# Adding the residual into the PSUM sums before the last slabs, with row sums on ScalarE and VectorE, in a three-layer mixer and expert network

## The chip, the cores and the metric

The kernel runs on one core of a Trainium2 chip. The metric is the device time of one execution in microseconds. TensorE does all the matrix products, VectorE and ScalarE the elementwise work, GpSimd a part of the splitting of weights, and SyncE issues every DMA.

## The reference

256 tokens of width 1024 pass through two Transformer-like layers with layer norm after each part, and then through a third layer with RMS norm. Each layer has a mixer and a PEER block, in which every token picks 8 x 16 of 16384 single-neuron experts.

```python
# first block: two layers, DN_ALPHA = 4 ** 0.25
h = layer_norm(DN_ALPHA * h + mix, ln_g[layer, 0], ln_b[layer, 0])
ffn = peer(h, w_q[layer], sub_keys[layer], u_tab[layer], v_tab[layer])
h = layer_norm(DN_ALPHA * h + ffn, ln_g[layer, 1], ln_b[layer, 1])
...
# second block: one layer, 16 meta tokens ahead of the 256
h = h + hybrid_mixer(rmsnorm(h, g_mix), ...)
h = h + peer_ffn(rmsnorm(h, g_ffn), ...)
h = rmsnorm(h, g_final)
```

So each of the six stages ends in a sum over a long inner dimension (`mix` or `ffn`), a residual, and a norm over the 1024 columns of each token. `layer_norm` takes the mean off, multiplies by the gain, divides by the root of the variance and adds the bias; `rmsnorm` has no mean and no bias.

## The kernel before

**Stages.** The six stages run one after the other: `ab`, `peer0`, `c`, `peer1`, `s`, `peer2`. The mixers are `ab`, `c` and `s`. Weights stream from HBM in slabs of 128x1024 floats through a ring of three buffers. For full precision each slab is split in two: ScalarE copies `ring` to `w_hi` (`split_lead`, L829), then GpSimd or VectorE forms `w_lo = ring - w_hi` (`split_rest`, L527). Activations are split likewise (`x_hi`, `x_lo`, or `c_hi`, `c_lo`), and each product is three matmuls: hi with hi (L576), hi with lo (L577), lo with hi (L578). A ring buffer may be refilled when its `w_lo` is ready, and `w_hi` rewritten when TensorE has counted the slab that used it (`slab_used`).

**Column slabs and row slabs.** Column slabs (`features`) are the weights that multiply x: 8 chunks x 3 matmuls of 256 columns into one bank `col`. Row slabs (`rows`) close a stage: for two token tiles t and two column halves they add 3 matmuls of 512 columns to each of the four PSUM banks `acc0` to `acc3`, 12 matmuls a slab. A stage ends with 8 (`ab_out`, `c_out`), 16 (`s_out`) or 128 (`v0` to `v2`) row slabs. In the last two slabs of a stage (`row_tail`) TensorE does tile 0 of both slabs first, then `acc2`, then `acc3`, so that tile 0 is full four bank sums ahead of the end.

**The joint between two stages.** When tile 0 is full, VectorE adds the residual to each bank (L1105, which also yields the row sum), forms the mean (L1129), multiplies the centred values by the gain in place in PSUM (L1137), and ScalarE sums the squares of the centred values (L889). Variance (L1141), root (ScalarE, L872), reciprocal (L1116) and the scaling with the bias into `h` (L1146) follow. TensorE transposes `h` (L664) into the `acc` banks, ScalarE copies them to `x_hi` (L865), VectorE forms `x_lo` (L1089), and the first column slab of the next stage can begin. TensorE fills the time with matmuls whose result nobody reads (`keep_busy`, L633). At the joint from `peer1` to `s`, RMS squares and scalings (L1212) of the new `h` come behind the layer norm, ahead of the transposes. Behind `s` and behind `peer2` only the RMS norm stands (`finish_rms`); there the residual is added into `h` in SBUF, and the squares are taken from `h`.

**Order.** Every engine runs its own program in written order. Nothing is scheduled at run time; semaphores join the engines. In the `v` slabs of a peer stage VectorE alternates `split_rest` and `coef_rest` (L1245, `c_lo`), while GpSimd is idle. In the mixers' row slabs GpSimd splits the weights, and VectorE makes `c_hi` and `c_lo` (`coef`, L1236 and L1238).

## Time and profile before

| | us |
|---|---|
| median of 3 runs | 2907.55 (2906.78 to 2907.93) |
| span of the profiled execution | 2904.1 |
| TensorE busy in it | 2869.2 (99%) |
| VectorE, ScalarE, GpSimd busy | 1934.1, 1562.2, 894.8 |

The page gives the span from the first to the last instruction; its own whole time isn't in it, and the median of the runs lies 3.45 us above the span. The page is read from the busy shares, through the waits of TensorE, to the timelines of single joints. The timeline gives for each instruction its start, its duration and the idle time in front of it with what ended that. A matmul's duration includes its passage through the array, so the distance between two starts tells its rate.

### The profile page before, as it was taken

The page shows a single profiled execution, that of the slowest core. Times are in us where ns is not written, and L with a number is a line of the kernel's source. Part 1 is how long each engine was busy: PE and PEld are TensorE (multiplying, and loading weights), DVE is VectorE, ACT ScalarE, POOL GpSimd, SP SyncE. Part 2 cuts the span into 40 slices and gives each one's busy share as a digit, 9 for nine tenths or more (in the row PEclk, how much of TensorE's full clock was granted, in tenths as well). Part 3 has the DMA queues.
Part 4 walks back from the last instruction along what each step waited for, and adds up shares of the span by engine and source line. Part 5 has one row for each costly group of instructions (what it writes and reads, how often), then busy time and mean ns, then how long its engine had stood idle before and what let it go on. Part 6 is the DMA issues. An engine that isn't in the chain of part 4 may idle for free.

```text
span 2904.1 us, 59734 instructions
## 1 busy us (share of the span) xinstructions
PE 2869.2 (99%) x21539; PEld 2620.1 (90%) x21539; DVE 1934.1 (67%) x3382; ACT 1562.2 (54%) x2548; POOL 894.8 (31%) x361
## 2 busy tenths in 40 slices
PE   8999999999999999999999999999999999999999
PEld 7899999888888889999998888889899999988887
DVE  4388577787556536947778855675539667788655
ACT  4444444677455554444467745554544544577554
POOL 3689600000004368970000000265779910000000
PEclk9999999999999999999999999999999999999999
DMA  6566655555765556665555576433565665555664
GB/s 214 163 184 184 185 168 172 173 176 174 240 192 158 151 160 182 184 185 170 170 174 174 175 238 192 151 128 127 164 192 181 182 181 167 173 175 176 207 193 161
DMA packets 146464, 515.20 MB, mean 177 GB/s; under 512 B 17552, under 2 KB 18576, under 8 KB 146336
## 3 DMA queue, kind: packets, MB, share of 16 engines
q1 hardware_dynamic: 146336, 513.46, 56.9%
q8 instruction: 85, 1.39, 0.2%
q14 instruction: 43, 0.35, 0.0%
HBM read 509.20 MB, written 4.19 MB: 177 GB/s over the span
## 4 chain that ended last, share of the span: by engine, by line
PE 90%; DVE 3%; ACT 2%; POOL 2%; issue 2%; DMA 1%; SPq 0%; DVEq 0%; ACTq 0%; POOLq 0%
PE col L576 15%; PE col L578 15%; PE col L577 15%; PE acc L576 13%; PE acc L578 13%; PE acc L577 13%; POOL w_lo L527 2%; PE col L723 2%; PE acc L723 2%; PE acc L683 1%; ACT w_hi L829 1%; ACT work L889 0%; PE acc L2301 0%; PE misc L2314 0%; DVE acc L1105 0%
## 5 line engine op out<-in xcount | busy, mean ns | idle before, releaser
L527 POOL TENSOR_TENSOR w_lo<-ring,w_hi 128x1024 fp32r<-128x1024 f32 x357 | 894.6, 2515 | 1442.5 <-ACT w_hi L829 1441.8
L829 ACT ACTIVATE w_hi<-ring 128x1024 fp32r<-128x1024 f32 x941 | 993.6, 1056 | 533.3 <-PE acc L578 439.3
L576 PE MATMUL col<-x_hi,w_hi 128*128 128x256 f32 (+1 forms) x3976 | 1125.0, 283 | 5.1 <-DVE x_lo L1089 3.6
L577 PE MATMUL col<-x_lo,w_hi 128*128 128x256 f32 (+1 forms) x3976 | 1118.9, 281 | 0.0
L578 PE MATMUL col<-x_hi,w_lo 128*128 128x256 f32 (+1 forms) x3976 | 1118.4, 281 | 0.0
L527 DVE TENSOR_TENSOR w_lo<-ring,w_hi 128x1024 fp32r<-128x1024 f32 x584 | 714.2, 1223 | 379.0 <-ACT w_hi L829 375.6
L576 PEld LDWEIGHTS col<-x_hi,w_hi 128*128 128x128 f32 x3976 | 750.7, 189 | 9.4 <-issue 6.2
L578 PEld LDWEIGHTS col<-x_hi,w_lo 128*128 128x128 f32 x3976 | 751.7, 189 | 0.0
L577 PEld LDWEIGHTS col<-x_lo,w_hi 128*128 128x128 f32 x3976 | 747.5, 188 | 0.7
L576 PE MATMUL acc<-w_hi,c_hi 128*128 128x512 f32 x1664 | 653.5, 393 | 1.0 <-issue 1.0
L578 PE MATMUL acc<-w_hi,c_lo 128*128 128x512 f32 x1664 | 648.3, 390 | 0.0
L577 PE MATMUL acc<-w_lo,c_hi 128*128 128x512 f32 x1664 | 647.3, 389 | 0.0
L836 ACT ACTIVATE work<-col 128x256 f32 (+1 forms) x464 | 178.7, 385 | 716.6 <-PE col L578 716.5
L578 PEld LDWEIGHTS acc<-w_hi,c_lo 128*128 128x128 f32 x1664 | 312.3, 188 | 66.0
L576 PEld LDWEIGHTS acc<-w_hi,c_hi 128*128 128x128 f32 x1664 | 312.5, 188 | 64.8 <-issue 1.5
L577 PEld LDWEIGHTS acc<-w_lo,c_hi 128*128 128x128 f32 x1664 | 312.6, 188 | 63.3
L1245 DVE TENSOR_TENSOR c_lo<-work,c_hi 128x256 fp32r<-128x256 f32 x390 | 165.5, 425 | 14.3 <-ACT c_hi L994 14.0
L994 ACT ACTIVATE c_hi<-work 128x256 fp32r (+1 forms) x384 | 153.6, 401 | 0.0
L1252 DVE MAX8 work<-work 128x8 f32<-128x128 f32 (+1 forms) x144 | 35.4, 323 | 166.1 <-ACT work L951 165.8
L1378 DVE SCALAR_TENSOR_TENSOR work<-acc,work 128x512 f32 (+1 forms) x96 | 61.9, 686 | 100.4 <-PE acc L723 100.4
L1367 DVE TENSOR_TENSOR h_tok<-mask_i,pairs_of_gate 128x2048 f16<-128x2048 f16 x96 | 123.7, 1288 | 0.2 <-issue 0.2
L999 ACT ACTIVATE h_tok<-iota_fp,neg_i 128x128 f16<-128x128 f16 x384 | 121.8, 388 | 0.2
(303 smaller groups left out, 1870.3 us busy)
## 6 DMA issues: line engine op xcount, KB each, us to landing
ring<-in_u SPq DMA_DIRECT2D x384, 512.0 KB, 3.7
ring<-in_v SPq DMA_DIRECT2D x384, 512.0 KB, 3.6
ring<-in_wq SPq DMA_DIRECT2D x48, 512.0 KB, 3.7
ring<-in_s_in SPq DMA_DIRECT2D x21, 512.0 KB, 3.4
ring<-in_c_in SPq DMA_DIRECT2D x16, 512.0 KB, 3.7
ring<-in_s_out SPq DMA_DIRECT2D x16, 512.0 KB, 3.3
...
```

The costliest lines, as they stand in the source:

```text
L527: eng.tensor_tensor(k.w_lo[s.slot][:, :], k.ring[s.slot][:, :], k.w_hi[s.slot][:, :].bitcast(F32), ALU.subtract).then_inc(k.lo[s.slot], 1)
L576: pe.matmul(out, a[0], b[0], start=start, stop=False, **kw)
L577: pe.matmul(out, a[0], b[1], start=False, stop=False, **kw)
L578: return pe.matmul(out, a[1], b[0], start=False, stop=stop, **kw)
L723: ins = pe.matmul(banks[t // HALF][:, t % HALF * EARLY:(t % HALF + 1) * EARLY], k.oh1[:, t, :], k.oh2[:, n, t, :], start=n == 0, stop=n == ...
L829: act.activation(k.w_hi[s.slot][:, :], k.ring[s.slot][:, :], ACT.Copy).then_inc(k.hi[s.slot], 1)
L836: act.activation(dst, src, func).then_inc(k.evac, 1)
L994: act.activation(k.c_hi[s.slot][:, :], act_of[:, s.index(values), :], ACT.Copy).then_inc(k.coef_h, 1)
L999: act.activation(k.oh1[:, t, :], k.iota_b[:, :], ACT.Abs, bias=k.neg_i1[:, at])\
L1245: dve.tensor_tensor(k.c_lo[s.slot][:, :], src, k.c_hi[s.slot][:, :].bitcast(F32), ALU.subtract).then_inc(k.coef[s.slot], 1)
L1367: dve.tensor_tensor(k.oh2.rearrange("p n t (i two) -> p n t i two", two=2), mask.unsqueeze(1).to_broadcast(shape), k.gate[:, bass.ds(b.ind ...
L1378: ins = dve.scalar_tensor_tensor(part, banks[half][:, :].rearrange("p (t i) -> p i t", t=HALF), 1.0 / GATE_UNIT, part, ALU.mult, ALU.mult)
```

## The change

Seven things are changed.

1. `ADDS` is 4 and `TAIL` is 6. In the last six row slabs of each stage, the four slabs ahead of the last two carry a mark 0 to 3. TensorE signals `bank_done` when bank number mark has been summed in that slab, and VectorE adds the residual into that bank right there, from PSUM to PSUM, and signals `resid`. TensorE waits for residual number n before its next sum into bank n: slab end-5 waits ahead of bank 0, slab end-4 ahead of bank 1, slab end-3 ahead of bank 2, and the tail ahead of bank 3.
2. On VectorE the residual n stands behind the splits or coefficients of slab end-4+n. It reads `h` from SBUF and the bank.
3. The loop over slabs on TensorE and on VectorE has one round fewer, and the slabs left stand behind it in straight order.
4. The row sums of banks 0, 1 and 3 come from ScalarE (a copy with an accumulator), that of bank 2 from VectorE (`tensor_reduce`).
5. Centring goes from PSUM to `h` in SBUF, and the scaling goes from `h` to `h`. The centring and scaling of the two tiles are interleaved. In `finish` ScalarE does tile 0's root between the tiles; ahead of `s` both further weight splits now stand behind the second root.
6. Behind `s` and `peer2` the squares and the RMS scaling read the banks; behind `s` VectorE also copies the banks into `h`.
7. The first column slab of a stage does its 16 products with `x_hi` first and its 8 products with `x_lo` last, with a wait for each part. There are fewer filler matmuls in a joint (8 and 8 in place of 12 and 20; 6 and 8 in place of 8 and 16 ahead of `s`).

```diff
+    def fresh_features(self, out, hi, lo, cols):
+        quads = (range(0, DC // 2), range(DC // 2, DC))
+        for quad, tiles in zip(quads, (3, 1), strict=True):
+            w.next(k.xhi, tiles)
+            for c in quad:
+                pe.matmul(out, hi[:, c, :], k.x_hi[:, c, cols], start=c == 0, stop=False)
+                pe.matmul(out, lo[:, c, :], k.x_hi[:, c, cols], start=False, stop=False)
+        for quad in quads:
+            w.next(k.x_ready, 2)
+            for c in quad:
+                ins = pe.matmul(out, hi[:, c, :], k.x_lo[:, c, cols], start=False, stop=c == DC - 1)
...
@@ def rows
+                bank = t * 2 + half
+                if mark and bank == mark - 1:
+                    self.w.next(k.resid)
...
+                if bank == mark and bank < ADDS - 1:
+                    ins.then_inc(k.bank_done, 1)
...
@@ def row_tail
-        self.row_slab(Slab(end - SLOTS))
+        for bank in range(begun, ADDS):
+            self.row_slab(Slab(end - TAIL + bank), mark=bank)
...
@@ def finish (ScalarE)
+        self.row_sum(0, 0)
+        self.row_sum(0, 1)
+        self.centred_squares(0)
+        self.w.next(k.tile_full)
+        act.wait_ge(k.used, end)
+        self.row_sum(1, 1)
+        self.tile_std(0, eps)
         if after != ("s",):
-            for t in range(NT):
-                self.centred_squares(t)
-            for t in range(NT):
-                self.tile_std(t, eps)
+            self.centred_squares(1)
+            self.tile_std(1, eps)
             self.split_lead(Slab(end + 1))
...
         else:
-            for t in range(NT):
-                self.centred_squares(t)
-                if t:
-                    self.tile_std(0, eps)
-                self.split_lead(Slab(end + 1 + t))
+            self.centred_squares(1)
             self.tile_std(1, eps)
+            for n in range(1, SLOTS):
+                self.split_lead(Slab(end + n))
             self.lead_meta()
...
@@ def residual (VectorE)
+        if bank < ADDS - 1:
+            self.w.next(k.bank_done)
+        else:
+            dve.wait_ge(k.used, last - 1)
...
+        dve.scalar_tensor_tensor(acc, h, alpha, acc, ALU.mult, ALU.add).then_inc(k.resid, 1)
...
@@ def layer_norm
         def centre(t, half):
-            self.w.next(k.sq)
-            dve.wait_ge(k.mean, means + t + 1)
-            acc = k.acc[t * 2 + half][:, :]
-            own.do(dve.scalar_tensor_tensor(acc, acc, k.small[:, 20 + t:21 + t], gain[:, half * 512:(half + 1) * 512],
-                                            ALU.add, ALU.mult))
+            if half == 0:
+                w.next(k.mean)
+                w.next(k.sq)
+            cut = slice(half * 512, (half + 1) * 512)
+            own.do(dve.scalar_tensor_tensor(k.h[:, t, cut], k.acc[t * 2 + half][:, :], k.small[:, 20 + t:21 + t],
+                                            gain[:, cut], ALU.add, ALU.mult))
...
-        def scale(t, half):
-            cut, acc = slice(half * 512, (half + 1) * 512), k.acc[t * 2 + half][:, :]
-            dve.scalar_tensor_tensor(k.h[:, t, cut], acc, k.small[:, 12 + t:13 + t], bias[:, cut], ALU.mult, ALU.add)\
-               .then_inc(k.rms_in if rms_next else k.h_part, 1)
+        def scale(t, half, after):
+            cut = slice(half * 512, (half + 1) * 512)
+            own.join(after)
+            dve.scalar_tensor_tensor(k.h[:, t, cut], k.h[:, t, cut], k.small[:, 12 + t:13 + t], bias[:, cut],
+                                     ALU.mult, ALU.add).then_inc(k.rms_in if rms_next else k.h_part, 1)
...
@@ def finish_rms
+        self.w.next(k.sq)
+        keep(0, 0)
+        self.mean_square(0, 1)
+        keep(0, 1)
+        self.w.next(k.sq)
+        keep(1, 0)
+        self.rms_norm(0, slot, summed=True)
+        self.mean_square(1, 1)
+        keep(1, 1)
+        self.rms_norm(1, slot, summed=True)
...
@@ MixAB.vector (the same line in MixC and MixS)
             e.coef(self.y[:, n, :], Slab(out + n))
+            if n >= 8 - ADDS:
+                e.residual(n - (8 - ADDS), out + 7, DN_ALPHA)
```

TensorE at slab 3 of the eight of `ab_out`, whose `w_hi1` it uses, between the transposes of `y` (L1579, now L1644). Before:

```order
L1579 MATMUL misc<-ident,work 128x128 [waits ret_y,ab_wide]
L1579 MATMUL misc<-ident,work 128x128 x3
L576 MATMUL acc0<-w_hi1,c_hi1 128x512 [waits lo_ready1,coef_ready1]
L577 MATMUL acc0<-w_lo1,c_hi1 128x512
L578 MATMUL acc0<-w_hi1,c_lo1 128x512
```

Now:

```order
L1644 MATMUL misc<-ident,work 128x128 [waits ret_y,ab_wide]
L1644 MATMUL misc<-ident,work 128x128 x3
L581 MATMUL acc0<-w_hi1,c_hi1 128x512 [waits residual_in_bank,lo_ready1,coef_ready1]
L582 MATMUL acc0<-w_lo1,c_hi1 128x512
L583 MATMUL acc0<-w_hi1,c_lo1 128x512
```

The slab's first matmul has a third semaphore to wait for, `residual_in_bank`.

VectorE in the same stretch. `c_hi2` and `c_lo2` in the first two rows are slab 4's coefficients, made from `y`, which TensorE transposes and ScalarE copies (`y_ready`). Before:

```order
L1236 CAST c_hi2<-work 128x256 [waits slab_used,y_ready]
L1238 TENSOR_TENSOR c_lo2<-work,c_hi2 128x256 [waits coef_hi_ready]
L1236 CAST c_hi0<-work 128x256 [waits slab_used]
L1238 TENSOR_TENSOR c_lo0<-work,c_hi0 128x256 [waits coef_hi_ready]
L1236 CAST c_hi1<-work 128x256 [waits slab_used,y_ready]
L1238 TENSOR_TENSOR c_lo1<-work,c_hi1 128x256 [waits coef_hi_ready]
L1236 CAST c_hi2<-work 128x256 [waits slab_used]
L1238 TENSOR_TENSOR c_lo2<-work,c_hi2 128x256 [waits coef_hi_ready]
```

Now:

```order
L1299 CAST c_hi2<-work 128x256 [waits slab_used,y_ready]
L1301 TENSOR_TENSOR c_lo2<-work,c_hi2 128x256 [waits coef_hi_ready]
L1159 SCALAR_TENSOR_TENSOR acc0<-h_tok,acc0 128x512 [waits slab_added_to_bank]
L1299 CAST c_hi0<-work 128x256 [waits slab_used]
L1301 TENSOR_TENSOR c_lo0<-work,c_hi0 128x256 [waits coef_hi_ready]
L1159 SCALAR_TENSOR_TENSOR acc1<-h_tok,acc1 128x512 [waits slab_added_to_bank]
L1299 CAST c_hi1<-work 128x256 [waits slab_used,y_ready]
L1301 TENSOR_TENSOR c_lo1<-work,c_hi1 128x256 [waits coef_hi_ready]
L1159 SCALAR_TENSOR_TENSOR acc2<-h_tok,acc2 128x512 [waits slab_added_to_bank]
L1299 CAST c_hi2<-work 128x256 [waits slab_used]
L1301 TENSOR_TENSOR c_lo2<-work,c_hi2 128x256 [waits coef_hi_ready]
L1159 SCALAR_TENSOR_TENSOR acc3<-h_tok,acc3 128x512 [waits slab_used]
```

Residual 0, which slab 3 on TensorE waits for, stands behind slab 4's coefficients; residuals 1 to 3 stand behind those of slabs 5 to 7.

VectorE at the end of the layer norm behind `c` (L1137, now L1184, is the centring; L1146, now L1201, the scaling). Before:

```order
L1137 SCALAR_TENSOR_TENSOR acc2<-acc2,small,work 128x512 [waits mean_ready,squares_ready]
L1137 SCALAR_TENSOR_TENSOR acc3<-acc3,small,work 128x512 [waits mean_ready,squares_ready]
L1141 TENSOR_SCALAR small<-small 128x1
L1116 RECIPROCAL small<-small 128x1 [waits std_ready,dve_step]
L1146 SCALAR_TENSOR_TENSOR h_tok<-acc0,small,work 128x512 [waits dve_step]
L1146 SCALAR_TENSOR_TENSOR h_tok<-acc1,small,work 128x512
L1116 RECIPROCAL small<-small 128x1 [waits std_ready]
L1146 SCALAR_TENSOR_TENSOR h_tok<-acc2,small,work 128x512 [waits dve_step]
L1146 SCALAR_TENSOR_TENSOR h_tok<-acc3,small,work 128x512
```

Now:

```order
L1195 RECIPROCAL small<-small 128x1 [waits std_ready]
L1201 SCALAR_TENSOR_TENSOR h_tok<-h_tok,small,work 128x512 [waits dve_step]
L1184 SCALAR_TENSOR_TENSOR h_tok<-acc2,small,work 128x512 [waits squares_ready,mean_ready]
L1190 TENSOR_SCALAR small<-small 128x1 [waits squares_ready]
L1201 SCALAR_TENSOR_TENSOR h_tok<-h_tok,small,work 128x512 [waits dve_step]
L1184 SCALAR_TENSOR_TENSOR h_tok<-acc3,small,work 128x512
L1195 RECIPROCAL small<-small 128x1 [waits std_ready]
L1201 SCALAR_TENSOR_TENSOR h_tok<-h_tok,small,work 128x512 [waits dve_step] x2
```

The four scalings read `h_tok` in place of a bank, and the first of them stands ahead of tile 1's centring.

ScalarE at the same joint (L829, now L860, writes `w_hi`; L889, now L928, squares; L872, now L903, takes the root). Before:

```order
L829 ACTIVATE w_hi0<-ring0 128x1024 [waits slab_loaded0,slab_used]
L889 ACTIVATE work,small<-acc0,small 128x512 [waits squares_ready,mean_ready]
L889 ACTIVATE work,small<-acc1,small 128x512 [waits squares_ready]
L889 ACTIVATE work,small<-acc2,small 128x512 [waits squares_ready,mean_ready]
L889 ACTIVATE work,small<-acc3,small 128x512 [waits squares_ready]
L872 ACTIVATE small<-small 128x1 [waits variance_ready] x2
L829 ACTIVATE w_hi1<-ring1 128x1024 [waits slab_loaded1,slab_used]
```

Now:

```order
L860 ACTIVATE w_hi0<-ring0 128x1024 [waits slab_loaded0,slab_used]
L910 ACTIVATE work,small<-acc0 128x512 [waits tile_summed_in_psum]
L910 ACTIVATE work,small<-acc1 128x512
L928 ACTIVATE work,small<-acc0,small 128x512 [waits squares_ready,mean_ready]
L928 ACTIVATE work,small<-acc1,small 128x512 [waits squares_ready]
L910 ACTIVATE work,small<-acc3 128x512 [waits slab_used,tile_summed_in_psum]
L903 ACTIVATE small<-small 128x1 [waits variance_ready]
L928 ACTIVATE work,small<-acc2,small 128x512 [waits squares_ready,mean_ready]
L928 ACTIVATE work,small<-acc3,small 128x512 [waits squares_ready]
L903 ACTIVATE small<-small 128x1 [waits variance_ready]
L860 ACTIVATE w_hi1<-ring1 128x1024 [waits slab_loaded1,slab_used]
```

Three row sums (L910) are new ahead of and between the squares; `w_hi1` follows the second root as before.

## Rows read from the trace of the kernel before

**Rows 1.** the page: busy us of each engine, share of the span

```profile
PE 2869.2 (99%) x21539; PEld 2620.1 (90%) x21539; DVE 1934.1 (67%) x3382; ACT 1562.2 (54%) x2548; POOL 894.8 (31%) x361
```

**Rows 2.** waits: TensorE line, its releaser, us in total, times, longest

```profile
PE acc L664 <- DVE h_tok L1146: 3.7, 6, 1.0
```

**Rows 3.** timeline, TensorE, joint c to peer1: start, duration, row, idle before

```profile
1045.79 1.48 PE L633 MATMUL col<-ident 128*128 128x256 bf16 x12
...
1050.95 1.31 PE L664 MATMUL acc<-ident,h_tok 128*128 128x128 f32 x8 [1.04 <-DVE h_tok L1146]
...
1054.62 0.36 PE L576 MATMUL col<-x_hi,w_hi 128*128 128x256 f32 x1 [0.85 <-DVE x_lo L1089]
```

**Rows 4.** timeline, VectorE at the same joint

```profile
1043.27 0.70 DVE L1105 SCALAR_TENSOR_TENSOR acc<-h_tok,acc 128x512 f32<-128x512 f32 x1 [4.49 <-PE acc L578]
...
1049.94 0.16 DVE L1116 RECIPROCAL small<-small 128x1 f32<-128x1 f32 x1
1050.14 1.41 DVE L1146 SCALAR_TENSOR_TENSOR h_tok<-acc,small,work 128x512 f32<-128x512 f32 x2
...
1051.65 1.41 DVE L1146 SCALAR_TENSOR_TENSOR h_tok<-acc,small,work 128x512 f32<-128x512 f32 x2
1052.98 2.69 DVE L1089 TENSOR_TENSOR x_lo<-acc,x_hi 128x512 fp32r<-128x512 f32 x4
```

**Rows 5.** timeline, ScalarE and then GpSimd at the same joint

```profile
1044.95 0.69 ACT L889 ACTIVATE work<-acc,small 128x512 f32<-128x512 f32 x1 [3.35 <-DVE small L1129]
...
1045.76 0.69 ACT L889 ACTIVATE work<-acc,small 128x512 f32<-128x512 f32 x1
...
1050.26 1.04 ACT L829 ACTIVATE w_hi<-ring 128x1024 fp32r<-128x1024 f32 x1
...
1053.15 1.25 ACT L865 ACTIVATE x_hi<-acc 128x512 fp32r<-128x512 f32 x2 [0.26 <-PE acc L664]
...
1051.38 2.36 POOL L527 TENSOR_TENSOR w_lo<-ring,w_hi 128x1024 fp32r<-128x1024 f32 x1 [7.30 <-ACT w_hi L829]
```

**Rows 6.** timeline, VectorE and then TensorE, fifth slab from the end of peer0

```profile
887.82 0.42 DVE L1245 TENSOR_TENSOR c_lo<-work,c_hi 128x256 fp32r<-128x256 f32 x1
...
888.02 0.39 PE L576 MATMUL acc<-w_hi,c_hi 128*128 128x512 f32 x1
```

**Rows 7.** timeline, ab_out slab 3: TensorE, GpSimd, VectorE

```profile
78.79 0.48 PE L576 MATMUL acc<-w_hi,c_hi 128*128 128x512 f32 x1
...
79.17 2.40 POOL L527 TENSOR_TENSOR w_lo<-ring,w_hi 128x1024 fp32r<-128x1024 f32 x1 [0.21 <-ACT w_hi L829]
...
80.25 1.46 DVE L1236 CAST c_hi<-work 128x256 fp32r<-128x256 f32 x1
81.75 0.43 DVE L1238 TENSOR_TENSOR c_lo<-work,c_hi 128x256 fp32r<-128x256 f32 x1
```

**Rows 8.** timeline, VectorE beside GpSimd, ahead of s and entering c

```profile
1850.77 1.27 DVE L1222 SCALAR_TENSOR_TENSOR work<-work,small 16x1024 f32<-16x1024 f32 x1
...
1851.56 2.74 POOL L527 TENSOR_TENSOR w_lo<-ring,w_hi 128x1024 fp32r<-128x1024 f32 x1 [556.97 <-ACT w_hi L829]
...
911.50 2.27 DVE L1953 TENSOR_TENSOR work<-work 128x8 f32<-128x8 f32 x1
...
911.34 2.40 POOL L527 TENSOR_TENSOR w_lo<-ring,w_hi 128x1024 fp32r<-128x1024 f32 x1 [1.70 <-ACT w_hi L829]
```

**Rows 9.** timeline, TensorE, joint peer1 to s

```profile
1854.24 0.66 PE L653 MATMUL misc<-ident,work 16*128 16x16 f32 x8
...
1867.82 0.36 PE L576 MATMUL col<-x_hi,w_hi 128*128 128x272 f32 x1 [0.84 <-DVE x_lo L1089]
```

**Rows 10.** windows: stretch, us, busy per engine (PE to POOL), clock, DMA

```profile
64.00:66.00 2.00, 2.00 (x6) 1.56 (x5) 1.05 (x3) 0.00 (x0) 0.00 (x0) 0.50 0.35 143
```

**Rows 11.** timeline, TensorE and then VectorE, the end of the kernel

```profile
2896.91 0.39 PE L578 MATMUL acc<-w_hi,c_lo 128*128 128x512 f32 x1
...
2900.28 1.42 DVE L1212 SCALAR_TENSOR_TENSOR work<-h_tok,small,work 128x512 f32<-128x512 f32 x2
```

More of the change, by code:

```diff
@@ L899, in tile_squares, with summed_squares @@
         self.tile_std(t)
+    def summed_squares(self, t, last):
+        k = self.k
+        for half in range(2):
+            if half == 0:
+                self.w.next(k.tile_full)
+            elif t:
+                self.act.wait_ge(k.used, last + 1)
+            self.square(k.acc[t * 2 + half][:, :], 2 * t + half)
+        self.tile_std(t)
     def finish(self, name, end):
@@ L1120, in layer_norm @@
         k, dve, own = self.k, self.dve, self.own
+        w = self.w
         gain, bias = view(k.big, G_AT[slot], D), view(k.big, G_AT[slot] + D, D)
-        means = self.w.count(k.mean)
-        def residual(t, half):
-            self.add_residual(t, half, last, DN_ALPHA, sums=True)
+        own.join()
         def minus_mean(t):
-            own.join()
+            w.next(k.sums, 2 if t == 0 else 2)
             dve.tensor_scalar(k.small[:, 20 + t:21 + t], k.small[:, 16 + 2 * t:17 + 2 * t],
@@ L1438, in peer @@
         at = first + EARLY + SLOTS
-        with dve.Fori(0, (VREST - SLOTS) // SLOTS) as i:
+        with dve.Fori(0, (VREST - SLOTS - ADDS) // SLOTS) as i:
             for p in range(SLOTS):
                 value(Slab(at + p, i))
-        for n in range(KEYS - (VREST - SLOTS) % SLOTS, KEYS):
-            value(Slab(first + n))
+        alpha = 1.0 if f"peer{layer}" in RMS_AFTER else DN_ALPHA
+        for bank in range(ADDS):
+            value(Slab(first + KEYS - ADDS + bank))
+            self.residual(bank, first + KEYS - 1, alpha)
 def vector_program(k, dve):
@@ L2099, in vector @@
             e.coef(yT, Slab(out + n))
+            if n >= 8 - ADDS:
+                e.residual(n - (8 - ADDS), out + 7, DN_ALPHA)
 class MixS:
```

136 lines of the change are left out of this document (74 added, 62 removed).

## Prediction

> **What bounds the kernel now.** I read the busy times first: TensorE works 2869.2 of 2904.1 us [rows 1], so time is lost or won only where TensorE stands still, in steps of a microsecond. The view of waits shows where: the transposes behind the four layer norms wait 3.7 us in all, six times [rows 2], in the joints between stages. So I laid the timelines of one joint side by side, and count in it from the start of the fillers, 1045.79, when the last slab has been fed; the first column slab starts at 1054.62, **8.83 us** on [rows 3]. The reader is to see in the rows that every link waits for the one before it, so that a link that moves by 0.1 moves the end by 0.1. The chain inside: residual from -2.52 (1043.27), reciprocal at 4.15, scaling of tile 0 at 4.35 and of tile 1 at 5.86, `x_lo` from 7.19 [rows 4]. From tile 1's scaling to its `x_hi` it is 1.50, and each `x_hi` takes 0.63 [rows 4, 5]. The joints behind `ab` and `peer0` repeat this within 0.1.
>
> **The joint after the change, times on the same count.** Residuals are already in, so ScalarE starts the row sums at -2.52. I price one at the 0.81 by which the squares follow each other [rows 5]: ended by -0.93. Mean, 0.25; tile 0's squares from -0.65 to 0.94; row sum of bank 3 to 1.75; mean; tile 1's squares from 2.02 to 3.61 (they cannot start before the last bank is summed). VectorE's small steps cost 0.12 to 0.2 each (reciprocal to scaling, 0.20 [rows 4]): variance 3.64, tile 0's second scaling 3.76, centring of bank 3 4.43, reciprocal 5.10, tile 1's scaling **5.29**, half a microsecond earlier than 5.86. With `x_hi` products first TensorE needs only the third `x_hi`: 5.29 + 1.50 + 0.63 + a restart. The restart lies between 0.06 (second scaling of a pair of 1.41 to the transposes) and 0.27 (second `x_lo`, 1054.35, to 1054.62) [rows 3, 4]; I take 0.2. That is 7.62 in place of 8.83: **a gain of 1.2** per layer norm if nothing else comes in. The `x_lo` parts no longer set the start: four of 0.67 behind the last scaling [rows 4] are done 1.8 after that start, and are first wanted when two thirds of the slab's 24 products are done.
>
> **The port.** Something does come in. ScalarE writes `w_hi` of the next slab right behind the second root: today at 1050.26, and GpSimd's split begins 1.12 later, 1051.38, and lasts 2.36 [rows 5]. After the change the root comes at 3.83, `w_hi` at 4.03, and GpSimd's split at 5.15 to 7.51, around tile 1's scaling at 5.29. Today that scaling runs under GpSimd's split unharmed, two in 1.41 [rows 4, 5], but it reads a bank and one SBUF tensor. Now it reads `h` and the bias, two SBUF tensors. Rows 8 show what such a pair does: VectorE's 128x8 sum of two SBUF tensors, begun 0.16 behind GpSimd's split, took 2.27 us and ended with it (913.77 against 913.74); and when VectorE's scaling of two SBUF tensors had begun first (1850.77 to 1852.04), GpSimd's split took 2.74 in place of 2.40 [rows 8]. The Trainium skill (SBUF — State Buffer, section Who interferes with whom) says that a VectorE instruction with two SBUF inputs contends with a GpSimd instruction that reads SBUF, and that the later one waits until the first has finished. By that rule centring into SBUF is what hurts in this change; the trace agrees in both directions.
> So tile 1's first scaling waits until 7.51 and the first matmul comes at 7.55 + 2.33 = 9.88: **1.05 slower** than now. If VectorE wins the race by 0.1, GpSimd gets in between its two scalings, the first quad starts at 7.6, but the second `x_hi` of tile 1 comes at 10.5, and the slab ends within 0.2 of the same time. The bounds of this term are -1.2 (no blocking) and +1.3. Three joints (behind `ab`, `peer0`, `c`): **+3.15**.
>
> **Ahead of s.** The same block holds tile 1's scaling; and both weight splits now stand behind the second root, so GpSimd has a second split waiting. VectorE's next instructions with two SBUF inputs (the sum of the squares, the second scaling) fall behind that one. Chain: scaling 7.5 to 8.15, GpSimd to 10.5, sum and variance 10.75, second scaling to 11.5, tile 0 normed 11.7 to 13.0, tile 1's squares end 12.6, its variance 13.2, normed from 13.8, first matmul at 13.8 + 2.33 = 16.15. Today it is 1867.82 - 1854.24 = 13.58 [rows 9]: **+2.6**. Without blocking the chain gives 13.35, -0.25; these are the bounds.
>
> **The wait in the peer stages.** Residual 0 stands on VectorE behind the coefficients of slab end-4. In `peer0` those begin at 887.82, and slab end-5, which must not touch bank 0 before the residual, begins at 888.02 [rows 6]. So TensorE stands: 887.82 + 0.38 (the next instruction starts at or just ahead of the end of one of 0.42) + 0.70 (the residual as now [rows 4]) + 0.2 restart = 889.10, **1.08**. In `peer1` and `peer2` the same two rows lie equally close. The later residuals have the cover of the slab that came late: residual 1 ends near 891.5, and bank 1 of the next slab is due a quarter into it, near 892.5. Three peer stages: **+3.25**. Bounds 2.7 and 3.6.
>
> **The wait in ab.** Here VectorE is late. Slab 3 begins on TensorE at 78.79. Residual 0 stands behind slab 4's coefficients, whose copy begins at 80.25 and is held to 81.71 by GpSimd's split (79.17 to 81.57), and whose `c_lo` begins at 81.75 [rows 7]. Residual 0: 82.10 to 82.80; slab 3 at 83.0 in place of 78.79: **4.2**. What hung on slab 3 moves along: the split of slab 6, the second transposes, `y_ready`, slab 6's copy (again behind a split), residual 2 at about 90.8 against bank 2 of slab 5, due at 90.65: 0.3. In sum **+4.5**; bounds 3.8 (the later copies find the port free) and 6.5 (one more split lies across). In `c` and `s` the coefficients come a third of a slab after the slab begins, and residual 0 is done 1 us ahead of its use: nothing.
>
> **Behind s and peer2.** At the end, the RMS scaling of tile 1 starts at 2900.28; the last matmul is issued at 2896.91, so the count begins at 2897.14 [rows 11], and it is 3.14. Now the squares start at -2.52 on the bank, tile 1's first ends at 0.4, tile 0 is scaled 0.6 to 1.9, tile 1 from 2.74: **-0.4**; GpSimd is idle there. Behind `s` three copies of 0.67 on VectorE take the gain and more, and `x_hi` first gives it back: 0, bounds -0.4 and +0.5. One loop round fewer costs nothing: its slabs are the same instructions. The fillers that are left out ran in time that had no other use.
>
> **The sum.** 3.15 + 2.6 + 3.25 + 4.5 - 0.4 = **+13.1 us**. It is made on the profiled span, 2904.1, and carried to the median, which lies 3.45 above it: 2907.55 + 13.1 = **2920.7**. A measurement of this kernel can tell about 0.2% (5.8 us) from no change: faster means below 2901.7, slower above 2913.4.
>
> **Rivals.**
> A. *The clock falls.* TensorE now stands 3.2 us in each layer norm joint, with fewer fillers before, and 4.0 in `ab`. At 64 to 66 us the granted clock is 0.50 (1.2 GHz), behind 32 small matmuls [rows 10]; while that lasts TensorE does half its work, so a fall of 2 to 4 us costs 1 to 2; I take 1.5. In one to five places: 2922 to 2928. For it: the gaps are three times the 1.04 that stands ahead of the transposes now [rows 3]. Against it: ahead of each gap the engine is busy without a pause. The Trainium skill (TensorE: Matmul & The Clock Gate, Part 1) says the gate follows how busy the engine has been; no run here shows a fall behind a plain gap. By the rule A is what would happen if the gaps count as idle. Chance 20% (two falls or more).
> B. *The port doesn't block a scaling.* Only the 128x8 sum was seen to wait, not this form. Then the joints give 3 x -1.2 and -0.25, and the two waits stay: +3.5, 2911, within 0.2%. 10%.
> C. *Not slower: the residuals don't hold TensorE and the port doesn't block.* VectorE would have to reach residual 0 ahead of the slab, that is 1.1 us earlier in the peers and 4.2 in `ab`; rows 6 and 7 speak against both. -3.6 - 0.25 - 0.4 = -4.3: 2903.3. It decides at 0 in both. 4%; 3% for a gain beyond 0.2% by something not seen here.
> D. *ab waits less or more* by 2: 2918 to 2923, inside the forecast.
>
> **How the numbers follow.** The forecast with its own width (2916 to 2923) 58%, A 20%, B 10%, C 4%, a gain 3%, beyond 2929 5%. The range takes in A and B: 2910.5 to 2928. Faster 0.03, the same 0.16 (B, C and the low edge), slower 0.81.
>
> **What would show it.** In the new profile: (1) TensorE idle for residuals once in each peer stage, about 1 us, and once in `ab` for 4 us; if VectorE's residual ends before the slab begins, those steps are wrong. (2) Scalings of 2.5 to 3 us in place of 0.7 while GpSimd splits, in four joints; if they take 0.7, B is right. (3) The first matmul 9.9 behind the last slab, 16 ahead of `s`. (4) Granted clock of 1.0 in all joints; a 0.5 gives A.

## The result, and the profile after

The changed kernel takes **2924.73 us** (median of five runs, 2921.02 to 2930.06) against 2907.55 (2904.75 to 2908.67) for the kernel before on the same chip: ratio 1.0063, 95% interval 1.0052 to 1.0074. It is slower by 17.2 us where the sum said 13.1; the time lies inside the range given, 4.0 us above the forecast. It is outside the forecast's own width (2916 to 2923) and inside that of rival A (2922 to 2928). The profiled execution is the longest of the five, 2930.06, with a span of 2928.2; so its difference to the span before, 24.1 us, holds more than the medians show.

TensorE's waits in the changed kernel, beside [rows 2] (TensorE line, its releaser, us in total, times, longest):

```profile
PE acc L690 <- DVE h_tok L1201: 12.1, 6, 2.9
PE acc L581 <- DVE acc L1159: 6.7, 5, 4.0
PE acc L690 <- DVE work L1275: 3.8, 4, 2.4
PE col L659 <- DVE h_tok L1201: 3.5, 1, 3.5
```

The wait behind the scalings (L690, which was L664) grew from 3.7 to 12.1 us, and the wait for residuals (L1159) is new. Joint behind `peer0`, TensorE, then VectorE, then GpSimd, to be laid beside [rows 3 to 5]:

```profile
912.54 1.05 PE L659 MATMUL col<-ident 128*128 128x256 bf16 x8
914.31 1.05 PE L659 MATMUL col<-ident 128*128 128x256 bf16 x8 [0.72 <-DVE small L1176]
...
917.12 0.66 PE L690 MATMUL acc<-ident,h_tok 128*128 128x128 f32 x4 [1.30 <-DVE h_tok L1201]
920.70 1.97 PE L690 MATMUL acc<-ident,h_tok 128*128 128x128 f32 x8 [2.93 <-DVE h_tok L1201]
```

```profile
916.32 0.74 DVE L1201 SCALAR_TENSOR_TENSOR h_tok<-h_tok,small,work 128x512 f32<-128x512 f32 x1
...
917.83 2.82 DVE L1201 SCALAR_TENSOR_TENSOR h_tok<-h_tok,small,work 128x512 f32<-128x512 f32 x1
```

```profile
917.76 2.34 POOL L532 TENSOR_TENSOR w_lo<-ring,w_hi 128x1024 fp32r<-128x1024 f32 x1 [6.88 <-ACT w_hi L860]
```

One line, L1201, takes 0.74 without GpSimd beside it and 2.82 when it starts 0.07 behind GpSimd's split. While TensorE stands for it, the granted clock falls (windows: stretch, us, TensorE busy, clock, DMA share, GB/s):

```profile
914.00:916.00 2.00, 1.51 (x12) 1.00 0.02 4
916.00:918.00 2.00, 0.66 (x4) 1.00 0.01 4
918.00:920.00 2.00, 0.00 (x0) 0.69 0.00 0
920.00:922.00 2.00, 1.30 (x6) 0.50 0.42 100
922.00:924.00 2.00, 2.00 (x10) 0.50 0.41 162
924.00:926.00 2.00, 2.00 (x13) 0.61 0.00 0
```

At 0.50 (1.2 GHz) the transposes take 1.97 in place of 1.31 and the first slab's products come every 0.21 us in place of 0.12. The same fall follows in the joints behind `ab` and `c`, ahead of `s`, and in `ab` at 82 to 90 us. One at 62 us is in the kernel before too, half as long. One more, inside `s` at 1929 to 1933, follows a wait for ScalarE that the change has no part in; the kernel before has that wait as well, and its clock stays at 1.0 there. TensorE inside `s`, changed and before:

```profile
1928.95 0.80 PE L2338 MATMUL acc<-ident,work 128*128 128x128 f32 x3 [3.07 <-ACT work L2446]
```

```profile
1907.00 0.55 PE L2269 MATMUL acc<-ident,work 128*128 128x128 f32 x3 [2.69 <-ACT work L2377]
```

TensorE in `ab`, where slab 3 stood at 78.79 before [rows 7], and at the fifth slab from the end of `peer0` [rows 6]:

```profile
79.77 0.63 PE L1644 MATMUL misc<-ident,work 128*128 128x128 f32 x4 [0.27 <-DVE work L1757]
84.38 0.76 PE L581 MATMUL acc<-w_hi,c_hi 128*128 128x512 f32 x1 [3.98 <-DVE acc L1159]
84.94 0.63 PE L582 MATMUL acc<-w_lo,c_hi 128*128 128x512 f32 x1
```

```profile
898.85 0.47 PE L581 MATMUL acc<-w_hi,c_hi 128*128 128x512 f32 x1 [0.81 <-DVE acc L1159]
```

Ahead of `s` the scaling and then a 128x1 sum are held, each by one of two splits in a row (VectorE, GpSimd):

```profile
1876.82 2.83 DVE L1201 SCALAR_TENSOR_TENSOR h_tok<-h_tok,small,work 128x512 f32<-128x512 f32 x1
1879.56 2.30 DVE L1258 TENSOR_TENSOR small<-small 128x1 f32<-128x1 f32 x1
```

```profile
1876.74 5.10 POOL L532 TENSOR_TENSOR w_lo<-ring,w_hi 128x1024 fp32r<-128x1024 f32 x2 [4.79 <-ACT w_hi L860]
```

**Where the 24.1 us of span went.** Five joints and the end are counted from the last row slab (start of the fillers; ahead of `s`, of the meta tokens' transposes) to the first column matmul; stages are what lies between.

| us | before | after | moved |
|---|---|---|---|
| joint ab to peer0 | 8.81 | 9.35 | +0.54 |
| joint peer0 to c | 8.91 | 10.06 | +1.15 |
| joint c to peer1 | 8.83 | 9.77 | +0.94 |
| joint peer1 to s | 13.58 | 15.75 | +2.17 |
| joint s to peer2 | 6.18 | 5.81 | -0.37 |
| behind the last slab | 6.96 | 6.39 | -0.57 |
| start and ab | 93.31 | 101.42 | +8.11 |
| peer0, c, peer1, s, peer2 | 799.50, 135.26, 799.62, 223.56, 799.58 | 801.77, 136.10, 803.43, 227.77, 800.58 | +12.13 |

Of the 20.2 us in the stages, the waits for residuals are some 7.5 (3.98 and 0.29 in `ab`, about 1.05 with the restart in each peer stage). The rest, nearly 13 us, has no wait of that size behind it; the windows show it as time at half clock. I add up, over all windows of 2 us, 2 us times what the clock lacks of 1.0, and call it the clock's deficit: 5.0 us before, **22.6** after. A part of it falls on time in which TensorE stands anyway and costs nothing; 0.8 to 3.3 us of each deficit lie behind the last matmul.

### The profile page after: what moved, and what is told of

The parts are those of the page before. It is cut to its first block, busy times and chain, and to the rows that moved or that the text cites. A ratio compares the mean times of both kernels' runs of the same rounds, so it can differ in the third digit from the quotient of the medians.

```text
span 2928.2 us, 59587 instructions
## 1 busy us (share of the span) xinstructions
PE 2876.2 (98%) x21481; PEld 2626.8 (90%) x21481; DVE 1942.7 (66%) x3374; ACT 1568.2 (54%) x2572; POOL 894.9 (31%) x361
## 3 DMA queue, kind: packets, MB, share of 16 engines
q8 instruction: 86, 1.41, 0.2%
## 4 chain that ended last, share of the span: by engine, by line
PE 90%; DVE 3%; POOL 2%; ACT 2%; issue 2%; DMA 1%; SPq 0%; DVEq 0%; ACTq 0%; POOLq 0%
PE col L581 15%; PE col L583 15%; PE col L582 15%; PE acc L581 13%; PE acc L583 13%; PE acc L582 13%; POOL w_lo L532 2%; PE col L749 2%; PE acc L749 2%; ACT w_hi L860 1%; PE acc L709 1%; DVE h_tok L1201 1%; PE acc L690 0%; DVE h_tok L1184 0%; PE acc L2370 0%
## 5 line engine op out<-in xcount | busy, mean ns | idle before, releaser
L860 ACT ACTIVATE w_hi<-ring 128x1024 fp32r<-128x1024 f32 x941 | 993.5, 1056 | 546.8 <-PE acc L583 455.8
L581 PE MATMUL col<-x_hi,w_hi 128*128 128x256 f32 (+1 forms) x3928 | 1111.8, 283 | 1.6 <-POOL w_lo L532 1.2
L582 PE MATMUL col<-x_lo,w_hi 128*128 128x256 f32 (+1 forms) x3928 | 1106.0, 282 | 0.0
L583 PE MATMUL col<-x_hi,w_lo 128*128 128x256 f32 (+1 forms) x3928 | 1105.5, 281 | 0.0
L581 PEld LDWEIGHTS col<-x_hi,w_hi 128*128 128x128 f32 x3928 | 742.4, 189 | 4.8 <-issue 2.9
L583 PEld LDWEIGHTS col<-x_hi,w_lo 128*128 128x128 f32 x3928 | 743.3, 189 | 0.0
L582 PEld LDWEIGHTS col<-x_lo,w_hi 128*128 128x128 f32 x3928 | 739.2, 188 | 0.7
```

What stands on the lines that cost most here:

```text
L581: pe.matmul(out, a[0], b[0], start=start, stop=False, **kw)
L582: pe.matmul(out, a[0], b[1], start=False, stop=False, **kw)
L583: return pe.matmul(out, a[1], b[0], start=False, stop=stop, **kw)
L860: act.activation(k.w_hi[s.slot][:, :], k.ring[s.slot][:, :], ACT.Copy).then_inc(k.hi[s.slot], 1)
```

## The experiments

Each ran in five rounds beside the kernel before (medians 2907.10, 2907.02 and 2908.16 in the three groups, the ratios each to its own). An interval is about 0.12% wide to either side, 3.5 us, so differences of one or two microseconds between the runs are read in the traces. Two groups differ by up to 1.1 us in the kernel before alone. A trace is one execution and has chance falls of the clock of its own: the one at 62 us lasts 6.8 us in some traces, 3.4 in others, and is missing in three. The joints, in us, in the order `ab`, `peer0`, `c`, `peer1`, `s`:

| kernel | median us, ratio (interval) | joints | deficit |
|---|---|---|---|
| before | 2907.55 | 8.81 8.91 8.83 13.58 6.18 | 5.0 |
| changed | 2924.73, 1.0063 (1.0052-1.0074) | 9.35 10.06 9.77 15.75 5.81 | 22.6 |
| e1 centring in PSUM | 2915.98, 1.0029 (1.0018-1.0039) | 7.24 7.53 7.70 15.31 5.81 | 10.4 |
| e10 late split | 2916.24, 1.0035 (1.0022-1.0049) | 7.25 7.98 7.67 15.75 5.81 | 15.0 |
| e6 order ahead of s | 2919.96, 1.0047 (1.0033-1.0060) | 9.49 10.06 9.77 11.16 5.80 | 16.3 |
| e4 fillers | 2916.88, 1.0035 (1.0023-1.0047) | 9.33 9.61 9.33 15.31 5.81 | 4.9 |
| e3 ab | 2920.08, 1.0044 (1.0030-1.0057) | 9.76 10.05 9.79 15.78 5.81 | 18.3 |
| e2 all residuals early | 2929.17, 1.0073 (1.0059-1.0087) | 9.78 9.08 9.78 15.76 5.80 | 18.9 |
| e7 residual 0 early | 2923.68, 1.0060 (1.0046-1.0074) | 9.78 10.06 9.78 15.78 5.80 | 17.9 |
| e9 before, fewer fillers | 2911.92, 1.0019 (1.0010-1.0029) | 9.29 9.55 8.83 14.34 6.17 | 11.0 |
| e11 before, x_hi first | 2903.74, 0.9988 (0.9979-0.9997) | 8.11 8.17 8.11 12.84 5.67 | 3.0 |
| e8 all mended | 2898.95, 0.9968 (0.9956-0.9980) | 7.23 7.54 7.25 11.15 5.80 | 2.8 |
| e12 e8, fewer fillers | 2904.66, 0.9987 (0.9978-0.9996) | 7.24 7.53 7.24 11.14 5.81 | 12.5 |

**Centring left in PSUM.**

```diff
-            own.do(dve.scalar_tensor_tensor(k.h[:, t, cut], k.acc[t * 2 + half][:, :], k.small[:, 20 + t:21 + t],
+            own.do(dve.scalar_tensor_tensor(k.acc[t * 2 + half][:, :], k.acc[t * 2 + half][:, :], k.small[:, 20 + t:21 + t],
...
-            dve.scalar_tensor_tensor(k.h[:, t, cut], k.h[:, t, cut], k.small[:, 12 + t:13 + t], bias[:, cut],
+            dve.scalar_tensor_tensor(k.h[:, t, cut], k.acc[t * 2 + half][:, :], k.small[:, 12 + t:13 + t], bias[:, cut],
```

> The changed kernel, but the centred values stay in the PSUM banks and the second scaling reads a bank and one SBUF tensor, as in the kernel before. All else, the order included, is the changed kernel. Theory (GpSimd's split holds every VectorE instruction with two SBUF inputs): the scalings take 0.7 us in place of 2.8 and 3.5 for a pair, the first column matmul stands 7.6 to 7.9 us behind the last row slab in place of 9.4 to 10.1 behind ab, peer0 and c, and 13.4 to 14.2 in place of 15.75 ahead of s. That is 3 x 2.1 + 2 = 8 us; TensorE's gaps shrink from 2.9 to under 1, so the falls of the granted clock at these four joints go too, 1 to 2 us each: 2924.7 - 8 - 4 = 2912.5 us (2909 to 2917). Rival 1 (the scaling is long because it reads what the centring has just written to SBUF, or for another reason that is not GpSimd): the same rows must be examined; if a two-SBUF instruction elsewhere beside a split is unharmed, this falls. Rival 2 (the fewer filler matmuls are what lowers the clock, not the gaps): joints shorten by 8 us, but the clock still falls: 2916.5 us.

At the joint behind `c`, VectorE and GpSimd:

```profile
1052.53 1.41 DVE L1201 SCALAR_TENSOR_TENSOR h_tok<-acc,small,work 128x512 f32<-128x512 f32 x2
```

```profile
1052.46 2.36 POOL L532 TENSOR_TENSOR w_lo<-ring,w_hi 128x1024 fp32r<-128x1024 f32 x1 [6.65 <-ACT w_hi L860]
```

The split begins 0.07 ahead of the scalings, as in the changed kernel, and two of them take 1.41. The three joints shorten by 2.1 to 2.5. Ahead of `s` the expectation was wrong, 15.31 for 13.4 to 14.2: the 128x1 sum, whose inputs lie in SBUF in either kernel, now meets the splits (2.18 us, in a wait of TensorE of 4.07). The clock still falls behind `c`, ahead of `s`, inside `s` and in `ab`, though not behind `ab` or `peer0`. Median 2915.98: inside the range written down, but no nearer to the theory's 2912.5 than to rival 2's 2916.5 (joints shorter, clock still falling), and the trace has some of each. In the trace 4.3 us of the difference are in `ab`, which the edit doesn't touch.

**The same block from the other side, and ahead of s.** In one run the weight copy that releases GpSimd moves behind tile 0's `x_hi` in three joints; in the other both copies ahead of `s` move behind the `x_hi` of tile 0 and of tile 1. Centring through SBUF stays in both.

```diff
-            self.split_lead(Slab(end + 1))
             self.lead_x([0])
+            self.split_lead(Slab(end + 1))
             self.lead_x([1])
```

> The changed kernel, with ScalarE's weight copy of the next slab, which releases GpSimd's split, moved behind the x_hi copies of tile 0 in the joints behind ab, peer0 and c. Centring and scaling still go through SBUF. Theory (GpSimd's split is what holds the scaling): the pair of scalings takes 1.4 us in place of 3.5, the first column matmul comes 7.2 to 7.8 us behind the zero in place of 9.4 to 10.1, the gap of 2.9 us falls under 1 us: 3 x 2.1 = 6.3 us, and the clock falls of three joints, about 1.5 us each, go or shrink: 2924.7 - 6.3 - 3 = 2915.4 us (2912 to 2918). Rival (two SBUF inputs alone make it long): the pair still takes 3.5 us, no gain. Rival 2 (w_lo of the second column slab is now late): a wait of up to 1 us at that slab takes half the gain.

```diff
-            for n in range(1, SLOTS):
-                self.split_lead(Slab(end + n))
...
-            self.lead_x(range(NT), at=META)
+            for t in range(NT):
+                self.lead_x([t], at=META)
+                self.split_lead(Slab(end + 1 + t))
```

> The changed kernel, with one thing moved on ScalarE at the joint from peer1 to s alone: the two weight copies that release GpSimd's splits stand behind the copies of x_hi of tile 0 and of tile 1, not behind the second root. VectorE's centring and scaling still read two SBUF tensors. Theory: with no split running there, the scaling of 2.83 us and the 128x1 sum of 2.30 us take 0.7 and 0.2, and ScalarE's squares no longer stand behind 2 us of copies; the first column matmul comes 11.4 to 12.5 us behind the zero in place of 15.75, and the granted clock stays at 1.0 there: 2924.7 - 3.8 - 1.7 = 2919.2 us. Rival 1 (two SBUF inputs are slow for another reason than GpSimd, say that the tensor was just written): the rows stay 2.8 and 2.3 us long. Rival 2 (w_lo then comes too late for the second column slab): TensorE waits at the second slab, gain 2 us or less.

VectorE behind `peer0` in the first, and ahead of `s` in the second:

```profile
914.13 1.42 DVE L1201 SCALAR_TENSOR_TENSOR h_tok<-h_tok,small,work 128x512 f32<-128x512 f32 x2
```

```profile
1875.07 0.75 DVE L1201 SCALAR_TENSOR_TENSOR h_tok<-h_tok,small,work 128x512 f32<-128x512 f32 x1
1875.74 0.15 DVE L1258 TENSOR_TENSOR small<-small 128x1 f32<-128x1 f32 x1
```

Two SBUF inputs alone cost nothing: it needs the split beside them. The joints come to 7.25, 7.98 and 7.67 in the first run and to 11.16 ahead of `s` in the second (expected 11.4 to 12.5), and no wait at the second column slab takes it back. In the first run the clock falls behind `peer0` and `c` all the same, 3.4 us long in place of 6.8; in the second it stays at 1.0 ahead of `s`.

**Fillers in the gaps.** 20 between the tiles' transposes in three joints, 20 and 18 more ahead of `s`:

> The changed kernel with more filler matmuls in the gaps: 20 between the transposes of the two tiles behind ab, peer0 and c (2.3 us at full clock, the gap there is 2.9), and ahead of s 20 and 18 more in the gaps of 3.6 and 2.4 us. VectorE, ScalarE and GpSimd are as in the changed kernel, so the chain of the norms is the same. Theory (gaps lower the clock): the first column matmuls stand where they did, 9.4 to 10.1 and 15.8 behind the zero, but the granted clock stays 1.0 at 918 to 926, 1064 to 1074 and 1884 to 1892 us, and the first slabs run at full rate: -1.5 to -2 us at each of four joints, 2924.7 - 6 = 2918.7 us. Rival (the clock falls for another reason, such as chip power or run to run chance): no change, 2924.7 us. Rival 2 (the fillers run into the transposes): slower by up to 1 us a joint.

```diff
-            self.keep_busy(14)
+            self.keep_busy(14 + 20)
...
-            self.keep_busy(12)
+            self.keep_busy(12 + 18)
...
             self.keep_busy(busy[t])
+            if normed and t and meta is None:
+                self.keep_busy(20)
```

TensorE behind `peer0`, and the windows:

```profile
914.25 2.35 PE L659 MATMUL col<-ident 128*128 128x256 bf16 x20
917.34 1.32 PE L692 MATMUL acc<-ident,h_tok 128*128 128x128 f32 x8 [0.75 <-DVE h_tok L1203]
918.78 0.36 PE L617 MATMUL col<-x_hi,w_hi 128*128 128x256 f32 x1
```

```profile
916.00:918.00 2.00, 1.25 (x10) 1.00 0.06 16
918.00:920.00 2.00, 1.88 (x14) 1.00 0.81 254
920.00:922.00 2.00, 2.00 (x19) 1.00 0.00 0
```

Nothing but products that nobody reads was added, and the median falls by 7.85 us, to 2916.88; the intervals don't meet. The clock stays at 1.0 in all four joints and in `s`; only 0.02 to 0.45 us a joint are from earlier first matmuls. So the clock cost the changed kernel near 2 us a joint in the medians. The two traces can't sharpen this: in this one the falls at 62 and at 82 us are half as long and the one inside `s` is missing, though no filler was added there.

**The wait in ab.** Residual 0 between the two halves of `y`, the others ahead of their slab's coefficients:

```diff
+            if pair == 0:
+                e.residual(0, out + 7, DN_ALPHA)
         for n in range(SLOTS + 1, 8):
+            if n > 8 - ADDS:
+                e.residual(n - (8 - ADDS), out + 7, DN_ALPHA)
...
-            if n >= 8 - ADDS:
-                e.residual(n - (8 - ADDS), out + 7, DN_ALPHA)
```

> The changed kernel, but in ab VectorE adds residual 0 between the two halves of the retention output, and residuals 1 to 3 ahead of the coefficients of slabs 5 to 7, not behind them. Theory: slab 3 no longer waits 3.98 us and slab 5 no longer 0.29; the chain to y is 0.7 us longer but not on TensorE's path until slab 6: -4.2 us, 2920.5. The granted clock of 0.5 at 82 to 90 us follows that wait, so it goes too, another 1.5 to 2.5 us: 2918.5 us. Rival 1: the clock of 82 to 90 us is a late answer to the many small matmuls before 70 us and stays: 2920.5. Rival 2: y comes later and slab 6 waits: the gain is less than 4.

```profile
78.76 0.63 PE L1644 MATMUL misc<-ident,work 128*128 128x128 f32 x4 [0.46 <-DVE work L1757]
79.36 0.47 PE L581 MATMUL acc<-w_hi,c_hi 128*128 128x512 f32 x1
79.67 0.40 PE L582 MATMUL acc<-w_lo,c_hi 128*128 128x512 f32 x1
```

Slab 3 follows the transposes by 0.60 in place of 4.61, its products come at full rate, and no window between 66 and 100 us is below 1.0. The wait and the fall behind it are gone; the median is 4.65 lower (1.6 less than expected), with intervals that overlap a little. The time alone would fit rival 1 (2920.5); its clock doesn't. Rival 2 holds in small: slab 6 starts 0.55 us behind the matmul ahead of it, waiting for its `c_lo`, near 0.4 us in all. The fall behind `ab`'s joint lasts longer here than in the changed kernel, which takes a part back.

**The residuals in the peer stages.** All four ahead of `value`, then residual 0 alone:

```diff
+            self.residual(bank, first + KEYS - 1, alpha)
             value(Slab(first + KEYS - ADDS + bank))
-            self.residual(bank, first + KEYS - 1, alpha)
```

> The changed kernel, but in the three peer stages VectorE adds residual n ahead of the split and the coefficients of slab end-4+n, not behind them. Theory: residual 0 then ends before slab end-5 begins, the three waits of 1.0 us go, and c_lo of slab end-4, 0.7 us later, is still a slab ahead of its use: 2924.7 - 3.0 = 2921.7 us. Rival (VectorE is the engine that sets the pace in the last slabs, so a residual costs its 0.7 us wherever it stands): the wait moves to the coefficients, no gain, 2924.7 us. A further rival (the late start of those slabs also lowers the clock): over 4 us.

VectorE and GpSimd at the last slab of `peer0` with all four moved, and TensorE two slabs from the end:

```profile
903.49 0.70 DVE L1159 SCALAR_TENSOR_TENSOR acc<-h_tok,acc 128x512 f32<-128x512 f32 x1 [1.24 <-PE acc L583]
904.09 1.22 DVE L532 TENSOR_TENSOR w_lo<-ring,w_hi 128x1024 fp32r<-128x1024 f32 x1
905.23 2.57 DVE L1308 TENSOR_TENSOR c_lo<-work,c_hi 128x256 fp32r<-128x256 f32 x1
```

```profile
904.68 2.83 POOL L532 TENSOR_TENSOR w_lo<-ring,w_hi 128x1024 fp32r<-128x1024 f32 x1 [555.50 <-ACT w_hi L860]
```

```profile
907.85 0.50 PE L581 MATMUL acc<-w_hi,c_hi 128*128 128x512 f32 x1 [3.04 <-DVE c_lo L1308]
```

A miss: 4.4 us slower in the medians (the intervals overlap) instead of 3.0 faster, and 3.35 us more for `peer0` in the trace. The first wait is gone, but the last residual waits for TensorE before the last slab's split may start, and in `peer0` the last `c_lo`, two SBUF inputs, is then caught by GpSimd's split. It takes 2.57, and TensorE stands 3.04; in `peer1` and `peer2` it stands 0.89 each for `c_lo`, in place of 0.81 for the residual. That much the first rival had (the wait moves to the coefficients, no gain); GpSimd's part in `peer0` stood nowhere.

```diff
+            if bank == 0:
+                self.residual(bank, first + KEYS - 1, alpha)
             value(Slab(first + KEYS - ADDS + bank))
-            self.residual(bank, first + KEYS - 1, alpha)
+            if bank:
+                self.residual(bank, first + KEYS - 1, alpha)
```

> The changed kernel, but in the three peer stages residual 0 alone stands ahead of the split and coefficients of slab end-4; residuals 1 to 3 stay behind theirs. Theory: the trace with all four moved ahead shows no wait for residual 0, and 3.0 us of wait for slab end-2, because residual 3 has to wait for a bank that is summed a slab later each time; with residual 0 alone moved neither wait is there: 2924.7 - 3.0 = 2921.7 us. Rival (the coefficients of slab end-3 become late, or the third slab from the end waits): no gain.

The long wait ahead of slab end-5 is gone in all three peer stages; there a matmul started 1.20 behind the one ahead of it, in place of 0.23. What is left, in `peer0` and `peer2`, is a short hold in slab end-4 ahead of bank 1, where residual 1 ends just then: two starts of 0.34, near 0.23 us in all. The median is only 1.05 lower, not 3.0, which the intervals can't tell from either; in the trace the peer stages win 1.35, 0.12 and 0.62. Why `peer1` keeps its length stays open; both kernels begin it with some 4 us at half clock.

**Fewer fillers in the kernel before.**

```diff
-        self.keep_busy(8 if before_s else 12)
+        self.keep_busy(6 if before_s else 8)
         self.w.next(k.mean, 2)
-        self.keep_busy(16 if before_s else 20)
+        self.keep_busy(8)
```

> The kernel before, with the smaller numbers of filler matmuls of the changed kernel (8 and 8 in place of 12 and 20; 6 and 8 in place of 8 and 16 ahead of s) and nothing else. Theory 1 (the long waits for GpSimd lower the clock): the gaps here grow from 1.0 to about 2.4 us each, shorter than 2.9, and the clock falls in some joints only: +0 to +3 us, 2907.6 to 2910.6. Theory 2 (every joint needs its fillers, whatever the chain does): falls at all four joints, 2 us each: 2915 us. Theory 3 (fillers have no part): 2907.6 us and clock 1.0 in all joints.

```profile
904.72 1.05 PE L633 MATMUL col<-ident 128*128 128x256 bf16 x8 [0.77 <-DVE small L1129]
908.13 3.38 PE L664 MATMUL acc<-ident,h_tok 128*128 128x128 f32 x16 [2.36 <-DVE h_tok L1146]
```

4.9 us slower, between theories 1 and 2; theory 3 falls. Gaps of 2.4 lowered the clock behind `ab` and `peer0` and ahead of `s`, not behind `c`, and 16 transposes took 3.38 in place of two times 1.31. The fillers were no idle pastime.

**x_hi first, alone, in the kernel before.** The edit is `fresh_features` as the change has it.

> The kernel before with part 7 of the change alone: the first column slab does its 16 products with x_hi first. Theory: the first column matmul waits for the third x_hi, not for the second x_lo: behind c 1053.15 + 0.63 + 0.2 = 1053.98 in place of 1054.62, that is -0.64 in each of three layer norm joints and ahead of s, -0.4 behind s: -3.0 us, 2907.0 - 3.0 = 2904.0 us. Rival (the x_lo products then wait, since x_lo ends 2.69 us behind its start): the slab ends when it ended, 2907 us.

```profile
1048.89 1.32 PE L680 MATMUL acc<-ident,h_tok 128*128 128x128 f32 x8 [0.20 <-DVE h_tok L1163]
1050.33 0.36 PE L612 MATMUL col<-x_hi,w_hi 128*128 128x256 f32 x1
```

Joints shorter by 0.70, 0.74, 0.72, 0.74 and 0.51, 3.4 in all where 3.0 was expected, and no wait inside the slab. The median of 2903.74 is 4.4 under the kernel before in the same group (2908.16), 3.5 by the ratio.

**Everything mended.** PSUM centring, residual 0 early in the peers, `ab` as above, the order ahead of `s`, and fillers in all remaining gaps (14 and 8 in front, 8 and 7 between the transposes; ahead of `s` 8, 26, 14 and 6).

> The changed kernel with every loss that the runs so far have shown mended at once: centring stays in PSUM, residual 0 stands ahead of the coefficients in the peer stages and between the halves of y in ab, the two weight copies ahead of s stand behind the copies of x_hi, and fillers cover the gaps. Theory, against the kernel before, by the joints of the single runs: behind ab, peer0 and c 7.2 to 7.5 us in place of 8.8 (3 x -1.4), ahead of s 11.2 in place of 13.6 (-2.4), behind s -0.4, at the end -0.6, slab 6 of ab +0.6: -7.0, so 2907.0 - 7.0 = 2900.0 us (2897 to 2904). Rival 1 (the losses overlap, so that the mended places turn into new waits): 2904 to 2908. Rival 2 (the extra fillers overrun at a lowered clock): a joint of 8.5 us and a fall of the clock in it.

```profile
905.90 1.04 PE L659 MATMUL col<-ident 128*128 128x256 bf16 x8
907.37 0.66 PE L694 MATMUL acc<-ident,h_tok 128*128 128x128 f32 x4 [0.43 <-DVE h_tok L1205]
907.86 0.93 PE L659 MATMUL col<-ident 128*128 128x256 bf16 x7
908.88 1.31 PE L694 MATMUL acc<-ident,h_tok 128*128 128x128 f32 x8
910.32 0.36 PE L617 MATMUL col<-x_hi,w_hi 128*128 128x256 f32 x1
```

**2898.95 us**, 0.32% (0.20 to 0.44%) faster than the kernel before, and faster than the changed kernel too. Against the kernel before in the same group (2908.16) that is -9.2 us, where -7.0 was expected from 2907.0. The trace shows -7.3 in the joints and -0.6 at the end, but reaches the transposes of `y` in `ab` 2.0 us later than the kernel before; why stays open. The joint lasts 7.54 with the clock at 1.0. The same with the changed kernel's fillers:

> The kernel with every loss mended, but with the fillers of the changed kernel (8 and 8; 6 and 8 ahead of s). It tells what the fillers are worth once the long gaps are gone: gaps of 0.7, 1.0 and 0.9 us remain in each joint. Theory 1 (gaps of about 1 us that follow each other lower the clock too, as in one joint of two in the run with centring in PSUM): 1 to 3 us slower than the mended kernel with fillers. Theory 2 (only a gap of 3 us does it): the same time within 0.5 us.

```profile
909.15 0.66 PE L690 MATMUL acc<-ident,h_tok 128*128 128x128 f32 x4 [1.30 <-DVE h_tok L1201]
910.66 1.67 PE L690 MATMUL acc<-ident,h_tok 128*128 128x128 f32 x8 [0.86 <-DVE h_tok L1201]
912.10 0.55 PE L617 MATMUL col<-x_hi,w_hi 128*128 128x256 f32 x1
```

```profile
910.00:912.00 2.00, 1.34 (x8) 0.87 0.00 0
912.00:914.00 2.00, 2.00 (x11) 0.50 0.37 84
```

Every joint is as long as with the fillers, to 0.01, and yet it takes 5.7 us more. The intervals touch (0.9980 and 0.9978), but the slowest of the six runs with fillers (2901.37) is faster than the fastest of the eleven without (2901.86). The clock falls behind `ab`, `peer0` and `c`, though no gap is over 1.30; theory 2 falls. In the traces the stages behind these three joints are 1.65, 1.24 and 1.32 us longer, 4.2 in all. A further 2.7 us is in `s`, where the clock falls behind a wait of 2.75 that no filler of this pair of runs touches, and `peer2` is 1.0 shorter. So more than theory 1's 1 to 3 us hangs on these fillers in the three joints of this trace; what the rest of the 5.7 is made of isn't shown.

## Why the prediction was right, and where it was not

**The port: right.** The pair of scalings took 3.48 (0.66 behind 2.82), the first matmul came at 9.35, 10.06 and 9.77 where 9.88 was given. Three joints cost +2.63, not +3.15, although the clock had fallen by then: tile 1's transposes began 7.88, 8.16 and 7.87 behind the zero, and took 1.77, 1.97 and 1.97. PSUM centring and the moved split each take the block away. The Trainium skill (SBUF — State Buffer, Who interferes with whom) says that a VectorE instruction with two SBUF inputs contends with a GpSimd instruction that reads SBUF. The traces agree for a 128x512 scaling (2.82 us for 0.74), a 128x1 sum (2.30 for 0.15) and `c_lo` (2.57 for 0.42). The gain of 1.2 without the block was sized low: 1.6, 1.4 and 1.1 in the first run, 1.4 to 1.6 in the mended kernel. Rival B is refuted.

**Ahead of s: right.** +2.17 for +2.6; the same two instructions are held, 2.83 and 2.30. The bound "without blocking, -0.25" was wrong: 11.16, that is -2.4, and most of the 2.2 us between them are ScalarE's two copies (1.99 us), which I left in that chain ahead of the squares; the run moved them as well, so the two effects aren't separated.

**The waits for residuals: right.** 0.81 idle, 1.05 with the slower starts around it, for 1.08, three times; in `ab` 3.98 and 0.29 for 4.2 and 0.3. Rival C needed them gone.

**The end and behind s.** -0.57 for -0.4, and -0.37 for 0: `x_hi` first gives 0.51 there by itself, so all the rest of the change costs 0.14 at this place.

Together these terms measure 2.63 + 2.17 + 3.15 + 4.3 - 0.57 - 0.37 = 11.3 us, for 13.1.

**What failed is the clock.** The sentence "The fillers that are left out ran in time that had no other use" and point (4), a clock of 1.0 in all joints, are wrong; rival A, at 20%, came true in all five places. It was priced at 1.5 each and measured near 2 (7.85 in four joints), and it came on top of the sum. 17.2 less 11.3 leaves 5.9 us for the clock in the median, and nearly 13 in the profiled execution, whose deficit is the largest seen. The case for it was in [rows 10] and in the gap three times as long; the case against, that TensorE works without a pause ahead of each gap, doesn't hold in the joints: waits of 0.72 and 1.30 stand ahead of the 2.93, with fewer fillers to cover them. With the fillers' 7.85 the terms as measured make 19.2; but 1.35 of these are the later first matmuls in the joints, which 2.63 and 2.17 hold already, so it is 17.8, near the 17.2. That the forecast of +13.1 fell so near is in part luck: terms sized 1.8 us too high stood in for a part of the clock.
